# First attention and gated scan placed between the units of the input projection, with one PSUM bank pair for the later groups

## What is computed

```python
def mixer_sublayer(x, ...):                       # x: 256 x 1024
    h = rmsnorm(x, ln1_g)
    proj = h @ w_in                               # 1024 x 5632
    q_sb, k_sb, v_sb, q_hg, f_hg, i_hg, g_hg, gate_sb, gate_hg = split(proj)   # 7 x 512, 2 x 1024
    y_sb = stick_breaking_attention(q_sb, k_sb, v_sb)       # 8 heads of 64
    f = lb + (1 - lb) * sigmoid(f_hg)
    o = hgrn2_chunk_scan(silu(q_hg), 1 - f, log(f), i_hg)   # 8 heads of 64
    o = o * rsqrt(mean(o * o) + EPS)
    y_hg = o * hg_norm_g * silu(g_hg)
    merged = sigmoid(gate_sb) * (y_sb @ w_branch_sb) + sigmoid(gate_hg) * (y_hg @ w_branch_hg)
    return x + merged @ w_out
```

## Time and profile before

| | |
|---|---|
| median of three runs | 1269.7 us |
| the profiled execution | 1269.43 us |
| its span, first to last instruction | 1267.4 us |
| mean granted TensorE clock (share of full) | 0.919 |
| TensorE busy | 1112.1 us, 88% |
| VectorE busy | 748.8 us, 59% |
| ScalarE busy | 613.3 us, 48% |
| GpSimdE busy | 35.8 us, 3% |
| weight units split by VectorE (line 855) | 204, mean 2288 ns |
| weight units split by ScalarE (line 495) | 204, mean 1913 ns |
| chain that ended last | TensorE 70%, VectorE 16%, ScalarE 8% |

### The profile page before, as it was taken

How to read it: one execution, slowest core, us unless ns; L and a number is a source line. 1 busy time by engine, 2 the same in 40 slices (tenths; PEclk the granted TensorE clock), 3 DMA queues, 4 the chain that set the end, 5 groups by cost and what they waited for, 6 DMA issues and landing times.

```text
span 1267.4 us, 13955 instructions
## 1 busy us (share of the span) xinstructions
PE 1112.1 (88%) x5353; PEld 914.4 (72%) x5353; DVE 748.8 (59%) x855; ACT 613.3 (48%) x714; POOL 35.8 (3%) x44
## 2 busy tenths in 40 slices
PE   5999687687499999999985999998898889999997
PEld 4788556576377777777764788887687767788886
DVE  4444225844657877878777455554538554555554
ACT  5454460033258778777774444342546334444341
POOL 0000013300000000000000000000000000000000
PEclk9999965798669999999997999998889769999999
DMA  8755111014148989889894865565232013555530
GB/s 285 256 191 197 67 51 49 17 34 161 61 166 295 316 308 340 316 318 334 308 346 142 300 197 175 190 199 166 96 104 67 1 34 100 166 194 176 192 100 34
DMA packets 116692, 223.29 MB, mean 176 GB/s; under 512 B 6118, under 2 KB 12381, under 8 KB 116638
## 3 DMA queue, kind: packets, MB, share of 16 engines
q1 hardware_dynamic: 112562, 216.76, 50.2%
q10 hardware_dynamic: 3708, 4.57, 1.1%
q0 software_dynamic: 368, 1.21, 0.3%
HBM read 221.45 MB, written 1.07 MB: 176 GB/s over the span
## 4 chain that ended last, share of the span: by engine, by line
PE 70%; DVE 16%; ACT 8%; issue 4%; ACTq 1%; POOL 0%; DMA 0%; DVEq 0%
PE ps L1571 16%; PE ps L1572 16%; PE ps L1573 16%; DVE w_lo L855 7%; PE ps L1816 4%; ACT w_hi L495 4%; PE ps L1817 4%; PE ps L1842 2%; PE ps L2048 2%; PE ps L1862 1%; DVE arena L991 1%; DVE y_lo L1232 1%; PE ps L2011 1%; ACT y_hi L683 1%; PE ps L1561 1%
## 5 line engine op out<-in xcount | busy, mean ns | idle before, releaser
L855 DVE TENSOR_TENSOR w_lo<-w_raw,w_hi 128x2048 fp32r<-128x2048 f32 x204 | 465.2, 2288 | 249.1 <-ACT w_hi L495 248.9
L495 ACT ACTIVATE w_hi<-w_raw 128x2048 fp32r<-128x2048 f32 x204 | 388.4, 1913 | 279.3 <-PE ps L1573 239.9
L1571 PE MATMUL ps<-w_hi,h_hi 128*128 128x512 f32 (+1 forms) x720 | 281.6, 391 | 16.1 <-DVE h_lo L882 7.5
L1572 PE MATMUL ps<-w_lo,h_hi 128*128 128x512 f32 (+1 forms) x720 | 279.0, 388 | 0.0
L1573 PE MATMUL ps<-w_hi,h_lo 128*128 128x512 f32 (+1 forms) x720 | 278.6, 387 | 0.0
L1571 PEld LDWEIGHTS ps<-w_hi,h_hi 128*128 128x128 f32 x720 | 139.3, 193 | 44.6 <-DVE h_lo L882 8.7
L1573 PEld LDWEIGHTS ps<-w_hi,h_lo 128*128 128x128 f32 x720 | 138.8, 193 | 26.9
L1572 PEld LDWEIGHTS ps<-w_lo,h_hi 128*128 128x128 f32 x720 | 138.9, 193 | 26.2
L1571 PE MATMUL ps<-w_hi,aT_hi 128*128 128x512 f32 x176 | 69.4, 394 | 7.8 <-DVE aT_lo L1140 6.0
L1572 PE MATMUL ps<-w_lo,aT_hi 128*128 128x512 f32 x176 | 69.0, 392 | 0.0
L1573 PE MATMUL ps<-w_hi,aT_lo 128*128 128x512 f32 x176 | 69.0, 392 | 0.0
(11 more groups left out here) (330 smaller groups left out, 1401.0 us busy)
## 6 DMA issues: line engine op xcount, KB each, us to landing
w_raw<-in_ffn_w_in SPq DMA_DIRECT2D x44, 1024.0 KB, 5.1
w_raw<-in_w_exp_gate SPq DMA_DIRECT2D x32, 1024.0 KB, 5.3
w_raw<-in_w_exp_up SPq DMA_DIRECT2D x32, 1024.0 KB, 6.5
w_raw<-in_w_exp_down SPq DMA_DIRECT2D x32, 1024.0 KB, 7.2
w_raw<-in_w_in SPq DMA_DIRECT2D x22, 1024.0 KB, 5.9
w_raw<-in_ffn_w_out SPq DMA_DIRECT2D x22, 1024.0 KB, 5.0
w_raw<-in_w_mix_in SPq DMA_DIRECT2D x8, 1024.0 KB, 5.2
w_raw<-in_w_out SPq DMA_DIRECT2D x4, 1024.0 KB, 5.1
```

What stands on the lines that cost most here:

```text
L495: act.activation(w_hi[:, u % SPLIT, :], w_raw[:, u % RAW, :], ACT.Copy).then_inc(hi_ready, 1)
L855: dve.tensor_tensor(w_lo[:, u % SPLIT, :], w_raw[:, u % RAW, :], w_hi[:, u % SPLIT, :], ALU.subtract).then_inc(lo_ready, 1)
L1571: pe.matmul(out, hi, w_h, start=first, stop=False)
L1572: pe.matmul(out, hi, w_l, start=False, stop=False)
```

## The change

TensorE's queue of the first sublayer is written anew, and the others follow it.

- `turn_stage` turns a staged group between units: q after unit 3, k after unit 4, the scan's q after unit 11, its f after unit 13. `logits(0)` stands behind unit 5. Then for each `ct`: `survive(ct)`, `logits(ct + 1)`, unit 8 + 2 ct, `values(ct)`, unit 9 + 2 ct. The diagonal follows unit 15, then unit 16, and each of the first five levels of `scores` has a unit (17 to 21) behind it. Unit 22 stands behind the seventh level, ahead of the far block; unit 23 stands behind the output products.
- The groups from i_hg on all use banks 6 and 7, so a group waits for the one before to leave. The logits have one bank pair (0, 1) in place of two.
- `qT` becomes two tensors, each zero in the 64 rows of the other head; `logits` and `survive` use all 128 rows of `kT`.
- `q_dec` is formed once a level, by a plain product; `scores` and the far block multiply 64 rows of it for each head, and write by head (`par`) where they wrote by token block.
- All seven groups of the attention and scan leave as plain copies; Silu and Sigmoid are applied later, on the turned `qhT` and `pre` and on `g_act`. The order of g_hg and f_hg is exchanged.
- The attention's result goes to `aT_hi` and `aT_lo`. Buffers in the arena move. GpSimdE's memset of `tok` moves to the start.
- VectorE's split of unit 25 and the gate products of units 22 and 23 stand ahead of the taking out of the scan's result (`h_lo`), where they stood behind it.

```diff
-IN_ORDER = ["q_sb", "k_sb", "v_sb", "i_hg", "q_hg", "g_hg", "f_hg", "gate_sb0", "gate_sb1", "gate_hg0", "gate_hg1"]
+IN_ORDER = ["q_sb", "k_sb", "v_sb", "i_hg", "q_hg", "f_hg", "g_hg", "gate_sb0", "gate_sb1", "gate_hg0", "gate_hg1"]
...
+        IN_BANK = {"q_sb": 6, "k_sb": 0, "v_sb": 2}
...
             softplus_parts(0)
-            softplus_parts(1)
-            split_hi(U_BRANCH)
+            split_hi(8)
+            split_hi(9)
             for ct in range(4):
+                leave_proj(3 + ct)
                 weights(ct)
-                if ct + 2 < 4:
-                    softplus_parts(ct + 2)
-                if ct in (1, 2):
-                    split_hi(U_BRANCH + ct)
+                if ct + 1 < 4:
+                    softplus_parts(ct + 1)
+                    split_hi(10 + 2 * ct)
+                    split_hi(11 + 2 * ct)
+            gate_of_hg(0, 1, qhT)
+            gate_of_hg(1, 2, pre)
+            split_hi(16)
             act.wait_ge(y_ready, 4)
-            act.activation(h_hi[:, 0:4, :].rearrange("p (b k) s -> p b (k s)", b=2), ps[:, 6:8, :], ACT.Copy).then_inc(ysb_hi, 1)
+            act.activation(aT_hi[:, :, :].rearrange("p (b k) s -> p b (k s)", b=2), ps[:, 4:6, :], ACT.Copy).then_inc(ysb_hi, 1)
+            split_hi(17)
+            for g in range(7, 11):
+                leave_proj(g)
+                split_hi(2 * g + 4)
+                if g < 10:
+                    split_hi(2 * g + 5)
+            act.wait_ge(proj_out, 7)
+            act.activation(g_act, g_act, ACT.Silu)
...
+            softplus(0)
+            split_lo(8)
+            split_lo(9)
+            for ct in range(3):
+                softplus(ct + 1)
+                split_lo(10 + 2 * ct)
+                split_lo(11 + 2 * ct)
+                if ct == 1:
+                    keep_T(3, qhT)
+                if ct == 2:
+                    dve.wait_ge(bias_stored, 32)
+                    keep_T(4, pre)
...
-                for par in range(2):
-                    i = dve.scalar_tensor_tensor(out=halves(q_dec[b][:, par, :], h)[:, :, 1, :], in0=halves(qh_f, h)[:, :, 1, :],
-                                                 scalar=half_rows[:, par:par + 1], in1=halves(pre_f, h)[:, :, 1, :],
-                                                 op0=ALU.mult, op1=ALU.mult)
-                i.then_inc(qdec_ready, 1)
+                dve.tensor_tensor(halves(q_dec[b], h)[:, :, 1, :], halves(qh_f, h)[:, :, 1, :], halves(pre_f, h)[:, :, 1, :],
+                                  ALU.mult).then_inc(qdec_ready, 1)
                 if level:
                     keep(level)
                 else:
+                    keep_ysb()
+                    split_lo(17)
                     keep_diagonal()
...
+                if level + 1 < LEVELS:
+                    split_lo(18 + level)
...
+            split_lo(U_BRANCH + 3)
+            for half in range(2):
+                cs = slice(512 * half, 512 * half + 512)
+                b0 = 6 - 6 * half
+                dve.wait_ge(unit_used, U_BRANCH + half + 1)
+                chain(dve.tensor_tensor(tok[:, :, cs], ps[:, b0:b0 + 2, :], gates[:, half], ALU.mult))
             dve.wait_ge(yhg_hi, 1)
...
+            def in_unit(u):
+
+                g, kh = u // 2, u % 2
+                b0 = IN_BANK.get(IN_ORDER[g], 6)
+                if g >= 4 and not kh:
+                    pe.wait_ge(proj_out, g)
+                unit(u, (b0, b0 + 1), 4 * kh, kh == 0, kh == 1)
...
+            in_unit(0)
+            in_unit(1)
+            in_unit(2)
+            bias_by_distance()
+            in_unit(3)
+            pe.wait_ge(bias_sb, 1)
+            turn_stage(0, 1, 4)
+            in_unit(4)
+            turn_stage(1, 2, 6)
+            in_unit(5)
             pe.wait_ge(sbT_ready, 2)
             logits(0)
-            logits(1)
-            pe.wait_ge(hgT_ready, 5)
+            in_unit(6)
+            in_unit(7)
+            pe.wait_ge(proj_out, 3)
             for ct in range(4):
                 survive(ct)
-                if ct + 2 < 4:
-                    logits(ct + 2)
+                if ct + 1 < 4:
+                    logits(ct + 1)
+                in_unit(8 + 2 * ct)
                 values(ct)
+                in_unit(9 + 2 * ct)
+                if ct == 1:
+                    pe.wait_ge(sp_ready, 3)
+                    turn_stage(2, 5, 0)
+                if ct == 2:
+                    pe.wait_ge(sp_ready, 4)
+                    turn_stage(3, 6, 0)
...
-                        q = q_dec[b][:, :, c0:c0 + P].rearrange("p e (n two h) -> p e n two h", two=2, h=h)[:, :, :, 1, :]
-                        i = pe.matmul(ps[:, 4 * (n % 2) + tt, ct * P:(ct + 1) * P], k_dec[:, b, ct, tt * P:(tt + 1) * P], q,
-                                      start=True, stop=True)
-                    i.then_inc(level_done, 1)
-
-            for level in range(LEVELS):
-                scores(level + 1)
+                        for par in range(2):
+                            r = slice(par * DH, (par + 1) * DH)
+                            q = q_dec[b][r, c0:c0 + P].rearrange("p (n two h) -> p n two h", two=2, h=h)[:, :, 1, :]
+                            i = pe.matmul(ps[:, 4 * (n % 2) + par, ct * DH + tt * S:ct * DH + tt * S + DH],
+                                          k_dec[r, b, ct, tt * P:(tt + 1) * P], q, start=True, stop=True)
+                            if tt == 1 and ct == 3:
+                                i.then_inc(level_done, 1)
+
+            in_unit(16)
+            pe.wait_ge(ysb_lo, 1)
+            for n in range(1, LEVELS):
+                scores(n)
+                if n < 6:
+                    in_unit(16 + n)
+            scores(LEVELS)
+            pe.wait_ge(proj_out, 11)
+            unit(U_BRANCH, (6, 7), 0, True, True, src=(aT_hi, aT_lo))
...
-            pe.wait_ge(ysb_lo, 1)
-            for half in range(2):
-                unit(U_BRANCH + half, (6 * half, 6 * half + 1), 0, True, True)
+            unit(U_BRANCH + 1, (0, 1), 0, True, True, src=(aT_hi, aT_lo))
```

## The result

The changed kernel takes 1211.8 us (median; 1208.05 to 1212.43) against 1269.3 for the kernel before, measured beside it: 0.954 of the time, 95% interval 0.9504 to 0.9576. The profiled execution took 1212.2 us with a span of 1210.4, 57.0 less than the span of before. The forecast was 1217.4 (1207 to 1240).

A forecast was written before the change was run, and what follows sets the result against it. TensorE's queue at full clock was taken as the bound: its terms from 18.2 us to unit 24 sum to 201.8 us, 52.3 less than 254.1, so 1269.4 becomes 1217.1, median 1217.4 us (range 1207 to 1240).

The forecast's parts named there:

- The bound: From 18.2 us to unit 24, TensorE at full clock becomes the bound throughout: 201.8 us in place of 254.1.
- unit 24 near 220: Sign expected in the profile: unit 24 starts near 220 us, where the kernel before had 272.3.
- Rival 4: Mixed stretches drop TensorE to 1.2 GHz and short work doubles: 1297 us; chance 0.06 in part, 0.05 in full.
- The attention: Between units on TensorE, four times each: turns 3.7 us in all, `survive` 12.4, `logits` 5.6, `values` 3.2.
- rival 2: `survive` and `logits` keep their 64-row prices: +6.1 + 2.7, 1226 us; chance 0.27 shared with rival 1.
- `scores`: Seven scan levels of 32 pieces, overlapping on opposite row halves: 2.2 us each (1.8 to 3.6), 15.4 in all.
- rival 1: In `scores`, 64-row pieces don't overlap: 3.6 us a level, 1225.7 us in all; chance 0.27 shared with rival 2.
- The wait for VectorE: In the scan, VectorE's level takes 7.8 (9.1) us against TensorE's 7.6; TensorE waits 3.5 (0 to 5).
- Hand-overs: Along TensorE's queue, about 45 changes of kind of work at 0.1 us: 4.5 us (nothing to 9).
- The bank pair: From group 4 on, waiting for the group before to leave banks 6 and 7 costs nothing; bare, 9 us.
- rival 3: In the scan, a late high half leaves steps unhidden: +10 us, 1228; chance 0.10 shared with a bare bank pair.
- The tail: Behind the scan: far scores 2.1 us, wait for their copy 1.3, output products 5.4, gap before unit 24 6.1.

The follow-up runs named there:

- The bare scan: Changed kernel with units 16 to 21 run ahead of the scan, so the diagonal and all levels of `scores` stand behind them: 1229.6 us, ratio 0.9699.
- the tail order with the shorter gap: Changed kernel with units 21 to 23 moved to where TensorE waits and first-block output products not waiting for the far scores' copy: 1200.6 us, repeated 1200.4.

## Why the prediction was right, and where its terms were not

**The bound.** TensorE as the bound throughout, at full clock: right, idle time 0 from 26 us to 190. Of the signs that the prediction gave, the clock at 1.00 to the end of unit 23 failed in the first profile and held in two more; unit 24 near 220 came at 213.5 and 210.1; TensorE's idle time in front of the seventh `scores` did not come at all. Rival 4 (mixed stretches drop the clock) is out for the stretches it meant; a fall came only in the output products, and cost 4.9 us there, where one through all mixed work would have cost 80. The argument that decided against it, that thin work in itself does not bring the clock down and the slow stretch of before had a long idle gap ahead of it, fits the output products issued twice (1.00) and one `q_dec` in the old order (0.50 from the start and never up). That a gap of 1.3 us could be followed by a fall was not in the prediction.

**The attention.** `survive` 3.07 (3.1), `logits` 1.23 (1.4), `values` 0.81 (0.8), turns 0.83 (0.93). The method was to take a pair of products in the earlier trace rows that was free of a change of rows and halve it. The experiment with 64 rows confirms the gain: 4.7 us for four steps where I had 6.1 + 2.7 for rival 2. Its price of `survive` was right (2 x 2.31 = 4.62, measured 4.61); it was too dear since it let `logits` carry changes of rows as well. They have none, and on halves side by side they are faster, 0.86.

**`scores`.** 2.2 forecast, 1.94 measured, 0.06 us a piece. The nearest row was the right one (two streams on opposite row halves) and rival 1 (3.6, as the earlier trace rows) is out. I had the pieces at two thirds of the logits' 0.10, and they are a little below that. That it is the alternation of the halves that makes them short shows in the same profile: the diagonal's pieces are 64 rows deep too, but one half's 16 stand behind one another, and they take 0.107 each (134.21 to 137.63), while the far scores, the same shape with the halves in turn, take 0.07 (16 in 1.16). The Trainium skill, "TensorEngine Tiling (Array Packing)", section "Tiling Modes", which lets different tiles load and multiply in parallel, is borne out: with the one-after-another pace of the output products (0.11 us a piece) 32 pieces would be 3.5 us, and two at a time 1.76, against 1.94. The rule of the Trainium skill, "TensorE: Matmul & The Clock Gate", section "LDWEIGHTS (loading the stationary operand)", a load by its columns, gave 3.4 a level by the prediction's estimate; the diagonal agrees with it (32 pieces, 3.42 us), `scores` doesn't. The bare scan shows that the same 32 pieces at half clock take 3.66.

**The wait for VectorE**, 3.5 forecast and 0 measured, is the step that failed; what was wrong in it is the account of VectorE's level. I had charged VectorE with all 2.7 us of GpSimdE's pair in each level. Half of that, the product into `k_dec` (1.30), is released by the same `scores` as `keep` and runs beside it; the other is stretched to 3.07 by the split, but two of these 3.07 us lie beside the split, and only what is left when `q_dec` starts (170.26 + 3.07 - 172.30 = 1.0) weighs on it. A level is then 1.23 + 0.62 + 2.21 + 1.6 = 5.7, not 7.8. The row that misled was the pair of `q_dec` of 3.33: what was in it of GpSimdE's work was contention between operations that overlapped, and I made of it a term of its own. The mechanism was real: with `q_dec` twice it is there, 4.96 us.

**Hand-overs.** 4.5 forecast for 45 breaks, about 2.9 measured (2.4 to unit 22, 0.2 or so at each of the last). They don't lie evenly. A unit between two kinds of 128 rows and 128 columns takes 5.56 us (44.14 to 49.70), 0.12 more than 5.44, all of it at its first product. Beside work on 64 rows or 64 columns it takes 5.62 to 5.68: that work also starts later behind its last product, 0.32 us (77.84 to 78.16) in place of 0.23.

**The bank pair.** No idle time in front of any even unit: free, as forecast. The run with the scan behind the units shows the price where nothing covers it, 1.35 us a group, as forecast too (1.3). And the late high half (rival 3) is absent too: the split of the level at 170.09 starts as soon as VectorE is free.

**The tail.** The far scores cost 1.16, not 2.1: the same overlap as `scores`, and below the lower bound of 2.0. The wait for the copy is 1.33 (1.3). Output products and unit 23 were 2.3 us each above the forecast in the first profile, from the clock alone: in the second they are 5.4 and 5.6. The gap before unit 24 is 5.97 there (6.1), and shrinks to 4.5 where the clock fell, since unit 23 then is what is late and `h_lo` waits for ScalarE's half (0.88 us at 211.75) instead of queueing behind the splits.

The profiled execution was forecast at 1217.1 and took 1212.2, 4.9 less. The sum was 6.4 too high: 3.5 the wait, 2.0 `scores`, 1.7 hand-overs, 0.9 the far scores, 1.5 the smaller terms and 1.6 the gap, less 4.6 for the clock and 0.2 for unit 22. Of it 1.9 came back behind unit 24; the last 0.4 are a start 0.1 earlier, the part of the time outside the span, and rounding. So the likeliest mechanism and its place were right, and errors of both signs, 11 us on one side and 7 on the other, made the total look better than its terms.

**What would be better still.** The change leaves 3.4 to 4.9 us of idle time before unit 24 and 1.33 before the output products. With the first removed and the second at 0.65 (the tail order with the shorter gap) the kernel takes 1200.5 us, 5.4% under the kernel before and 9.5 to 11.3 us under the changed kernel's two medians.

## What to carry to other kernels

Where one stage fills an engine and the next one leaves it idle in a chain of short steps, interleave them, and price the result as that engine's queue at full clock: every thin kind of work from a start-to-start distance, plus 0.1 to 0.2 us for each dense block that stands between thin ones. Charge contention between two engines once, on the one that ends last, and look which of the partner's operations really stand in line and which run in a wait that is there anyhow. Where a buffer is given up for the new order, price the wait that the order covers; it comes back as soon as the order changes. A saving on one engine of a bare chain (3 us for one `q_dec` a level) and an order that needs it (9 us when it is taken back) are worth more together than apart.

## What the runs showed of the hardware that was not expected

- The granted clock inside the same stretch of the same program differed between executions: 0.50 from 196 us on in one profile, 1.00 in two others, each behind an idle gap of 1.33 us. It made unit 24 3.4 us later.
- TensorE stayed at 0.50 from 205 us to 249.5, busy nearly all the time with thin products (one `q_dec` in the old order), and at 1.00 for 164 us of mixed work once it had been brought up by units. A larger busy share did not go with a higher clock: the kernel before had 0.94 with TensorE 46% busy.
- 64-row pieces on alternating row halves cost 0.06 us each at full clock (64 columns) and 0.07 (128 columns); on the same half in succession 0.107, as much as the 128-row ones of the output products (0.11).
- VectorE's 128x2048 split stretches a 128x512 operation of GpSimdE from 1.58 to 3.04 us and keeps its own 2.28; a `q_dec` of VectorE that starts while GpSimdE's operation lasts goes from 0.69 to 1.58. In most of these pairs the one that started later was the longer; at 142.93 it was not (0.67, and 4.11 for GpSimdE's).
